# Moving one unit of the output projection forward, and three half updates of x from VectorE to GpSimd, in a two-layer decoder trunk

## The reference, cut to what matters

```python
def rms_norm(x, g):
    y = x * lax.rsqrt(jnp.mean(x * x, axis=-1, keepdims=True) + NORM_EPS)
    return y * g

for i in range(DEPTH):
    hn = rms_norm(x, norm_gains[i, 0])
    y = mixer(hn)                            # ends in o @ w_out
    x = x + rms_norm(y, norm_gains[i, 1])    # output norm 1 (i = 0), 3 (i = 1)
    hn = rms_norm(x, norm_gains[i, 2])
    f = conv_ffn(hn)                         # ends in h @ w_down
    x = x + rms_norm(f, norm_gains[i, 3])    # output norm 2 (i = 0), 4 (i = 1)
    gate = jax.nn.sigmoid(rms_norm(x, ple_norm_g[i]) @ ple_gate_w[i])
    x = x + gate * (p[i] @ ple_proj_w[i])
```

## Time and profile before

| what | us |
|---|---|
| time before, median of 3 runs | 1519.74 (1519.41 to 1519.96) |
| the profiled execution's own time | 1518.93 |
| its span in the trace | 1517.1 |
| PE busy in the span | 1463.6 |

### The profile page before, as it was taken

How to read it: one execution, slowest core, us unless ns; L and a number is a source line. 1 busy time by engine, 2 the same in 40 slices (tenths; PEclk the granted TensorE clock), 3 DMA queues, 4 the chain that set the end, 5 groups by cost and what they waited for, 6 DMA issues and landing times.

```text
span 1517.1 us, 23491 instructions
## 1 busy us (share of the span) xinstructions
PE 1463.6 (96%) x7566; PEld 1217.1 (80%) x7566; DVE 720.8 (48%) x1256; ACT 719.5 (47%) x1308; POOL 686.0 (45%) x982
## 2 busy tenths in 40 slices
PE   6999998999999999999999999999999999999998
PEld 5877766888888888887978787888888888888886
DVE  5477772644434300246476767674644343410053
ACT  5245545654444423357365646464744444423262
POOL 4634436365656555364420202111465556555452
PEclk9999999999999999999999999999999999999999
DMA  5321113233232322242410101010142222232221
GB/s 202 121 70 57 55 43 110 85 102 106 85 108 85 109 97 97 70 141 84 162 49 10 56 9 48 14 41 28 61 135 96 97 97 97 97 100 95 97 97 56
DMA packets 37563, 127.80 MB, mean 84 GB/s; under 512 B 6144, under 2 KB 6912, under 8 KB 37248
## 3 DMA queue, kind: packets, MB, share of 16 engines
q1 hardware_dynamic: 32256, 117.45, 23.2%
q10 hardware_dynamic: 5248, 9.55, 1.8%
HBM read 124.90 MB, written 2.10 MB: 84 GB/s over the span
## 4 chain that ended last, share of the span: by engine, by line
PE 58%; issue 16%; POOL 16%; DVE 5%; ACT 4%; POOLq 0%; ACTq 0%; DVEq 0%
PE banks_a L1215 22%; POOL w_lo L297 16%; PE banks_b L1224 9%; PE banks_a L1224 8%; PE banks_a L1621 4%; PE banks_b L1215 4%; PE banks_a L1192 4%; PE banks_b L1593 2%; PE banks_b L1379 1%; DVE nm L951 1%; PE banks_a L1398 1%; ACT w_hi L361 1%; PE banks_a L1512 1%; ACT y L364 1%; PE banks_b L1596 0%
## 5 line engine op out<-in xcount | busy, mean ns | idle before, releaser
L297 POOL TENSOR_TENSOR w_lo<-w_raw,w_hi 128x256 fp32r<-128x256 f32 x864 | 656.7, 792 | 766.5 <-ACT w_hi L361 766.2
L361 ACT ACTIVATE w_hi<-w_raw 128x1024 fp32r<-128x1024 f32 x216 | 228.5, 1061 | 277.4 <-PE banks_b L1224 132.6
L1215 PE MATMUL banks_a<-nT_lo,w_hi 128*128 128x512 f32 (+1 forms) x968 | 342.9, 376 | 1.0 <-DVE nT_lo L804 1.0
L1215 PE MATMUL banks_a<-nT_hi,w_hi 128*128 128x512 f32 (+1 forms) x968 | 343.6, 376 | 0.0
L1215 PE MATMUL banks_a<-nT_hi,w_lo 128*128 128x512 f32 (+1 forms) x968 | 341.8, 374 | 0.0
L1215 PEld LDWEIGHTS banks_a<-nT_lo,w_hi 128*128 128x128 f32 x968 | 174.1, 190 | 32.3 <-DVE nT_lo L804 1.2
L1215 PEld LDWEIGHTS banks_a<-nT_hi,w_lo 128*128 128x128 f32 x968 | 173.7, 189 | 32.1
L1215 PEld LDWEIGHTS banks_a<-nT_hi,w_hi 128*128 128x128 f32 x968 | 173.8, 189 | 31.6
L857 DVE SCALAR_TENSOR_TENSOR y<-banks_a,conv,y 128x511 f32<-128x511 f32 x88 | 66.0, 750 | 219.7 <-ACT y L466 219.2
L466 ACT ACTIVATE y<-banks_a,conv 128x512 f32<-128x512 f32 x88 | 68.5, 779 | 209.2 <-PE banks_a L1215 209.1
L704 ACT ACTIVATE gp<-banks_b,nm 128x128 f32<-128x128 f32 (+3 forms) x128 | 67.5, 527 | 49.3 <-DVE nm L951 43.5
(11 more groups left out here) (256 smaller groups left out, 2395.3 us busy)
## 6 DMA issues: line engine op xcount, KB each, us to landing
w_raw<-in_w SPq DMA_DIRECT2D x216, 512.0 KB, 3.2
g_pre<-in_gains ACTq DMA_DIRECT2D x6, 512.0 KB, 4.8
x<-in_x SPq DMA_DIRECT2D x4, 512.0 KB, 9.4
g_post<-in_gains ACTq DMA_DIRECT2D x4, 512.0 KB, 5.8
out<-x SPq DMA_DIRECT2D x4, 512.0 KB, 2.6
pe_raw<-in_pT ACTq DMA_DIRECT2D x2, 512.0 KB, 5.2
w1k<-in_w ACTq DMA_DIRECT2D x1, 1024.0 KB, 4.8
w1v<-in_w ACTq DMA_DIRECT2D x1, 1024.0 KB, 6.8
```

The source lines that it names most:

```text
L297: pool.tensor_tensor(w_lo[slot][:, cols], w_raw[k % RAW][:, cols], w_hi[slot][:, cols].bitcast(F32), ALU.subtract).then_inc(S["w_lo_done"], 1)
L361: act.activation(w_hi[u % RING][:, :], w_raw[u % RAW][:, :], ACT.Copy).then_inc(S["w_hi_done"], 1)
L1215: m = pe.matmul(bank[:, cols], w[:, k * P:(k + 1) * P], r[:, k, cols], start=(k, pas) == (0, 0), stop=(k, pas) == (KT - 1, 2))
```

## The change

It has two parts. The first touches layer 0's output projection alone: the unit that was its last comes fifth in the stream, and PE takes it for all four tiles right behind the first four units; tiles 2 and 3 then take the other three units. The accumulation's first and last step of tiles 2 and 3 move with it, and the fifth unit's slot is released once tile 3 has used it. The second part touches all four output norms: for tiles 0 to 2 POOL does the first half of x, with a multiplication in place (`y0` by the tile's scale) and an addition, as soon as DVE signals the reciprocal (`yrec_done`). For tile 3 DVE does it as before, after POOL is through with tile 2. POOL does this between the low parts of a projection's last unit and those of the next block's first unit, so its one loop over units 30 to 215 becomes five stretches.

```diff
+            def first_halves(r):
+                for t in range(TT - 1):
+                    pool.wait_ge(S["yrec_done"], 4 * r + t + 1)
+                    cols = y0[:, t, :]
+                    link(pool.tensor_scalar(cols, cols, yst[:, 2, t:t + 1], None, ALU.mult))
+                    pool.tensor_tensor(x[:, t, 0:HALF], x[:, t, 0:HALF], cols, ALU.add).then_inc(S["xfirst_done"], 1)
...
-            lows(late + 2, UNITS)
+            at = late + 2
+            for r, end in enumerate(PLAN[n] for n in ("up0", "gate0a", "up1", "gate1a")):
+                lows(at, end)
+                first_halves(r)
+                at = end
+            lows(at, UNITS)
...
                 def update(t):
                     dve.wait_ge(S["ystd_done"], 4 * r + t + 1)
-                    link(dve.reciprocal(yst[:, 2, t:t + 1], yst[:, 1, t:t + 1]))
                     scale = yst[:, 2, t:t + 1]
-                    dve.scalar_tensor_tensor(x[:, t, 0:HALF], y0[:, t, :], scale, x[:, t, 0:HALF], ALU.mult, ALU.add)\
-                        .then_inc(S["xfirst_done"], 1)
+                    signal(dve.reciprocal(scale, yst[:, 1, t:t + 1]), "yrec_done", 4 * r + t + 1)
+                    if t == TT - 1:
+                        dve.wait_ge(S["xfirst_done"], 4 * r + t)
+                        dve.scalar_tensor_tensor(x[:, t, 0:HALF], y0[:, t, :], scale, x[:, t, 0:HALF], ALU.mult, ALU.add)\
+                            .then_inc(S["xfirst_done"], 1)
                     link(dve.scalar_tensor_tensor(A[t], A[t], scale, g_post[:, HALF:D], ALU.mult, ALU.mult))
...
             by_unit(U, range(4), B, oT0_hi, oT0_lo, KT, last_head)
+            weights(U + 5)
             for t in range(TT):
-                for n in range(7 if t < 2 else 4, 8):
-                    weights(U + n + 1)
+                m = of_tiles(U - 3, 7, (t,), A, oT0_hi, oT0_lo, KT, ends=(0, KT - 1) if t < 2 else (6, 5))
+                if t < 2:
+                    m.then_inc(S["tile_done"], 1)
+            m.then_inc(S["units_done"], 1)
+            for t in (2, 3):
+                for n in range(4, 7):
+                    weights(U + n + 2)
                     if t == 3 and n == 4:
                         pe.wait_ge(S["y0_done"], 4)
                         transposes(1, 0)
-                    if t == 3 and n == 7:
+                    if t == 3 and n == 6:
                         transposes(1, 1)
-                    m = of_tiles(U, n, (t,), A, oT0_hi, oT0_lo, KT)
-                    if t == TT - 1:
+                    m = of_tiles(U + 1, n, (t,), A, oT0_hi, oT0_lo, KT, ends=(6, 5))
+                    if t == 3:
                         m.then_inc(S["units_done"], 1)
-                if t < TT - 1:
+                if t == 2:
                     m.then_inc(S["tile_done"], 1)
...
         if layer == 0:
             units.append(wo[4:7])
+            wo = wo[[0, 1, 2, 3, 7, 4, 5, 6]]
```

More of the change, by code:

```diff
@@ L227, in trunk @@
         std_done xn_done xT_done nhi_done nlo_done x_updated
-        ysq_done y0_done ystd_done xfirst_done v_done
+        ysq_done y0_done ystd_done yrec_done xfirst_done v_done
         qrope_done krope_done scores_done negmax_done probs_done mix_done mixT_done ovar_done orinv_done pT_done pv_done
@@ L1217, in features, with tokens @@
                 return m
-            def tokens(bank, slot, c, lhs_hi, lhs_lo, kk, t, n_k, passes=range(3)):
+            def tokens(bank, slot, c, lhs_hi, lhs_lo, kk, t, n_k, passes=range(3), ends=None):
+                first, last = ends or (0, n_k - 1)
                 for pas in passes:
@@ L1224, in tokens @@
                     m = pe.matmul(bank[:, :], a[:, kk, tok(t)], w[:, c * HALF:(c + 1) * HALF],
-                                  start=(kk, pas) == (0, 0), stop=(kk, pas) == (n_k - 1, 2))
+                                  start=(kk, pas) == (first, 0), stop=(kk, pas) == (last, 2))
                 return m
@@ L1234, in by_unit, with of_tiles @@
                     of_tiles(U, n, range(TT), banks, lhs_hi, lhs_lo, n_k).then_inc(S["units_done"], 1)
-            def of_tiles(U, n, tiles, banks, lhs_hi, lhs_lo, n_k, passes=range(3)):
+            def of_tiles(U, n, tiles, banks, lhs_hi, lhs_lo, n_k, passes=range(3), ends=None):
                 for c in range(2):
@@ L1240, in of_tiles @@
                     for t in tiles:
-                        m = tokens(banks[t], (U + n) % RING, c, lhs_hi, lhs_lo, kk, t, n_k, passes)
+                        m = tokens(banks[t], (U + n) % RING, c, lhs_hi, lhs_lo, kk, t, n_k, passes, ends)
                 return m
```

## The result

The changed kernel takes 1532.09 us (median of 4 runs, 1531.64 to 1533.52) against 1519.85 for the kernel before: a ratio of 1.0079, 95% interval 1.0066 to 1.0091, so 12 us slower. The forecast was 1525.8 with a range from 1520 to 1530. Its profiled execution took 1533.52 us with a span of 1531.7, 14.6 more than the span before.

A forecast was written before the change was run, and what follows sets the result against it. Each output norm was taken to end with the chain through ACT and DVE, not PE. Losses of 2.6 + 1.0 + 1.5 + 1.0 = 6.1 us on 1518.93 gave 1525.0, plus 0.8 for the median: 1525.8, range 1520 to 1530.

The forecast's parts named there:

- The failed step: All four output norms, tiles 0 to 2: POOL's 512-column multiplication takes 0.80 us, bounds 0.20 and 1.47.
- The pair's own upper bound: POOL's multiplication, idle gap and addition per tile: 0.80 + 0.08 + 1.28 = 2.16 us, bounds 1.32 and 3.02.
- a pair of 2.40: Multiplication at 1.04 us, gap 0.08, addition 1.28: +2.9 on the forecast, 1528.7; used for the range's upper end.
- The rest of the sum: Addition 1.28 us, gap 0.08; losses of 2.6, 1.0, 1.5 and 1.0 us in the four output norms.
- the prediction's own rate: In each output norm, every 0.1 us more in POOL's pair costs 0.3 us.
- the rival of the quick pair: All output norms: a pair of 1.64 us gives 1521.3, the 1.32 floor 1520.1, so no clear change; chance 20%.
- The rival that won by it: Layer 0's output projection: PE's 4.0 us stall is on the path; first norm gains 6.6 us, total 1516.6; chance 8%.
- The rival of PE's clock: Behind the first norm: PE's new idle time halves its clock, 2.4 us more, 1528.2; chance 12%.
- The low parts: Next block's first weight units queue behind tile 2's pair on POOL: costed at nothing, up to 1 us uncovered in first norm.
- The marks: Signs in the changed profile: no PE `w_lo` wait before fifth unit, pairs of 0.8 and 1.28 us, ACT and PE waits.

The follow-up runs named there:

- prices: Kernel before, plus eight POOL instructions on an unread buffer behind its last low part; at 512 columns scalar multiplication 1.57 us, broadcast product 1.04.
- pool_only: Changed kernel with the old unit order, so only POOL's first halves remain; 1532.97 us, 1.0077 of the kernel before.
- mul_broadcast: Changed kernel with POOL's multiplication written as a tensor_tensor product with the scale broadcast; 1525.52 us, 1.0036 of the kernel before.
- pool_two: Changed kernel, but POOL does the first halves of tiles 0 and 1 only, DVE those of 2 and 3; 1528.6 us, 1.0064.
- quarter: Changed kernel, but POOL takes 256 columns of each first half with the broadcast product, DVE adds the other 256; 1519.97 us, 1.0000.
- order_only: Changed kernel without POOL's first halves: only the new unit order, DVE updates all first halves; 1519.04 us, 0.9988 of the kernel before.
- shadow: New unit order, DVE updates all first halves; POOL does comparable work for tiles 0 to 2 on an unread scratch tile; 1523.8 us, 1.0020.
- table_only: Kernel before, with ACT's root table load moved in front of the wait for the banks B; 1520.06 us, 0.9992.

## Why the prediction was wrong

**The failed step** is a term of the sum: "The multiplication reads one tensor only: half the slope gives 0.74, the broadcast product 1.04; I take 0.80, bounds 0.20 and 1.47." It measured 1.57, alone as well as in the norms, outside the bounds too. The assumption that one operand less makes a POOL instruction cheaper had no row behind it; the bounds were made of other instructions' prices, and nothing kept the price below them. The pair's own upper bound, 3.02, did cover the 2.94 that were measured, but the range stopped at a pair of 2.40. The Trainium skill, GPSIMD Engine Reference, section 4.1, calls one-input instructions on GpSimd roughly line-rate; this case's rows, 1.49 and 1.57 us for 512 columns against 1.29 for an addition of two tensors, don't agree.

**The rest of the sum held.** The addition was forecast at 1.28 and took 1.29, the gap 0.08. With 2.94 for 2.16, the prediction's own rate of 0.3 us a norm for 0.1 us of the pair adds 2.3 to each norm: 4.9, 3.3, 3.8 and 3.3. Measured were 4.57 (4.85 less the 0.28 us by which the first norm starts earlier), 3.23, 4.36 and 3.21: 15.4 in all against 15.3. The clock gives 1.5 back behind the first norm. That leaves 13.9 of the 14.6. The other 0.7 lies between the second norm's last transposes and the third norm's first square, 1079.36 - 664.04 = 415.32 against 414.60 before; prices, which is the kernel before up to there, takes 415.42, so single executions of one kernel differ by as much. The third norm loses 1.1 us more than the second, of which the sum had 0.5. The other 0.6 stands where PE's clock falls: in the change, with a granted clock of 0.90 from 1080 to 1090 and 0.93 from 1090 to 1100, and in pool_only, with 0.89 and 0.94, the third norm lasts 29.45 us and the fourth 28.84 and 28.85; in mul_broadcast and pool_two, with 1.00 there, the third lasts 27.22 and 27.79 and the fourth 27.21 and 27.75. That fits the clock as the cause, but no run changed the clock alone.

**The rate held for smaller pairs too, but not the total.** For a pair of 2.40 the prediction gave 1528.7; mul_broadcast, at 2.41, is 1.0036, some 5.5 us and not 9. Inside its norms it loses 3.20, 1.57, 2.13 and 1.58 us, 8.5 in all, and from its pair to the change's 0.1 us costs 0.31 in the first, second and fourth norm. The difference lies outside the norms: in its kept execution the clock gives 1.5 back behind the first norm, which the sum had at nothing, and its first square stands at 264.94, 0.83 earlier and not 0.31: 8.5 - 1.5 - 0.8 = 6.2, and its span, 1523.4, is 6.3 longer. At a pair of 1.50 (quarter) the norms lose 0.59, 0.04, 0.49 and 0.04 us and the time is the same as before, as the rival of the quick pair said; that rival was right in its mechanism and lacked the price.

**What bounds the kernel** was read rightly. PE's 4.0 us wait was not on the path: without it (order_only) the kernel gains 0.12%. The rival that won by it falls. (The prediction calls it the longest single one. PE waits longer once, 9.5 us for `xn` before its first transposes, at the start of the kernel before, where the change does nothing.) The rival of PE's clock falls as the cause as well: the clock does drop around PE's new waits in the first norm, but the second and the fourth norm lose 3.2 us each at a granted clock of 1.00 (620 to 670 and 1430 to 1480), and pool_only, in the old order, is as slow as the change.

**The low parts**, "I cost this at nothing", cost PE 0.9 us in the first norm under the cover of the late `xn`, so the step held. Its price without that cover, "up to 1 us in the first norm", was too low: in shadow one wait alone was 3.31, though the work for tile 2 held POOL for 3.82 us there (278.62 to 282.44) and a pair takes 2.94.

**The marks** that were to show it came, but for the multiplication's 0.80 and the sizes of the norms' losses: POOL as releaser before ACT's squares (3.40 us against the 2.6 forecast), PE's wait for `xn` before the first transposes (4.8 against 4), no wait for `w_lo` before the fifth unit.

## What to carry to other kernels

Price an instruction by its own form or not at all: when the trace has no row of it, look whether the same arithmetic can be written in a form that has one (here the product with a broadcast operand, 1.04 us where the scalar form takes 1.57). A step on a chain that is walked twelve times makes twelve times its error, so the least certain price on such a chain sets the range. And before an instruction is moved to relieve an engine, look for the gap that it is to fill: the table load took nothing off the chain when it moved within a full stretch of ACT, and 6.66 - 5.14 = 1.5 us when it moved one instruction further (in the trace; the kernel's time, 0.9983, is not told apart from order_only's 0.9988).

## What the runs showed of the hardware

GpSimd's multiplication of one tensor by a scale per partition costs 2.50 ns a column, the product of two operands 1.66 and the sum of two tensors 2.16 (from 256 and 512 columns each).

VectorE and GpSimd hold each other up when VectorE reads two tensors from SBUF. Beside VectorE's addition of x and `y0`, GpSimd's 256 columns took 1.49 us instead of 0.92 (shadow); in quarter GpSimd's product kept its 0.61 and VectorE's 256 columns took 0.94, more than its 512 alone. Beside an instruction of VectorE with one operand in PSUM and one in SBUF (L838 of the changed kernel) GpSimd's 1.57 was the same as alone. The Trainium skill, SBUF — State Buffer, section "Who interferes with whom", says that an instruction of VectorE with two SBUF inputs contends with one of GpSimd that reads SBUF, that one with at most one SBUF input, outside VectorE's 2-port modes, doesn't, and that the order of issue decides who blocks. The rows agree with the first two. Who came first they don't settle: by its start VectorE is ahead in both runs, by 0.07 us in shadow (266.01 against 266.08) and by 0.05 in quarter (631.75 against 631.80), and no run has VectorE's 256 columns alone.

What a fall of PE's clock costs where PE is busy shows between the first norm's last transposes and the second norm's first square. The kept executions of the kernel before, prices and table_only have a granted clock of 0.83 from 290 to 300 and take 340.4 us; the change, order_only, pool_only and mul_broadcast have 1.00 there and take 338.9. The difference is 1.5 us, where 10 x 0.17 is 1.7.
